# Attention scores of two heads together on the two halves of the array's rows, and bias addition with row maximum in one VectorE instruction

## What is computed

```
DILATED_PATTERNS = ((128, 1), (512, 4), (2048, 16))
def dilated_mixture_attention(q, k, v):
    outs, lses = [], []
    for window, dilation in DILATED_PATTERNS:
        o, lse = dilated_window_attention(q, k, v, window, dilation)
        ...
    wts = jax.nn.softmax(jnp.stack(lses, axis=0), axis=0)
    o = jnp.sum(wts[..., None] * jnp.stack(outs, axis=0), axis=0)
```

## Time and profile before

| | |
|---|---|
| median of 3 runs | 2277.92 us (2269.21 to 2280.78) |
| the profiled execution: time | 2277.48 us |
| the profiled execution: span | 2275.9 us |
| TensorE matmul busy | 2167.8 us (95% of the span) |
| VectorE, ScalarE busy | 1007.0 us, 633.6 us |
| mean granted TensorE clock | 0.98 |
| attention, first scores to last values matmul | 1215.3 to 1406.1 us |

### The profile page before, as it was taken

How to read it: one execution, slowest core, us unless ns; L and a number is a source line. 1 busy time by engine, 2 the same in 40 slices (tenths; PEclk the granted TensorE clock), 3 DMA queues, 4 the chain that set the end, 5 groups by cost and what they waited for, 6 DMA issues and landing times.

```text
span 2275.9 us, 25468 instructions
## 1 busy us (share of the span) xinstructions
PE 2167.8 (95%) x10465; PEld 1797.1 (79%) x10465; DVE 1007.0 (44%) x1109; ACT 633.6 (28%) x876; POOL 814.8 (36%) x320
## 2 busy tenths in 40 slices
PE   2999999999999999799999998979999999999998
PEld 2788888888877688678886787867888888878886
DVE  5776665666354456652504765142000000025656
ACT  4344444444210112322004755032000000012212
POOL 2333323323333355424541000333444444445552
PEclk9999999999999999989997999989999999999999
DMA  9111011011111111421110000321111111111131
GB/s 361 33 38 38 28 37 37 28 37 34 41 47 47 38 46 56 166 70 52 46 46 19 1 1 4 118 92 62 50 46 46 47 55 46 46 46 46 46 117 77
DMA packets 129974, 130.31 MB, mean 57 GB/s; under 512 B 6310, under 2 KB 103031, under 8 KB 128888
## 3 DMA queue, kind: packets, MB, share of 16 engines
q1 hardware_dynamic: 123208, 113.08, 15.5%
q10 hardware_dynamic: 6704, 16.36, 1.9%
HBM read 116.84 MB, written 12.58 MB: 57 GB/s over the span
## 4 chain that ended last, share of the span: by engine, by line
PE 91%; DVE 4%; ACT 3%; issue 1%; DMA 1%; ACTq 0%; DVEq 0%
PE psum L395 15%; PE psum L397 14%; PE psum L396 14%; PE psum L415 10%; PE psum L416 10%; PE psum L417 10%; PE psum L526 3%; PE psum L810 3%; PE psum L799 2%; PE psum L789 1%; PE psum L640 1%; PE psum L445 1%; DMA arena<-x 1%; DVE arena L1604 1%; PE psum L790 1%
## 5 line engine op out<-in xcount | busy, mean ns | idle before, releaser
L373 POOL TENSOR_TENSOR w_hi<-w_raw,ones 128x1024 fp32r<-128x1024 f32 x158 | 382.4, 2420 | 1422.3 <-PE psum L397 754.3
L395 PE MATMUL psum<-h_hi,w_hi 128*128 128x512 f32 x1472 | 586.9, 399 | 1.6 <-POOL w_lo L376 1.1
L397 PE MATMUL psum<-h_hi,w_lo 128*128 128x512 f32 x1472 | 575.3, 391 | 0.0
L396 PE MATMUL psum<-h_lo,w_hi 128*128 128x512 f32 x1472 | 574.7, 390 | 0.0
L376 POOL TENSOR_TENSOR w_lo<-w_raw,w_hi 128x1024 fp32r<-128x1024 f32 x158 | 432.4, 2737 | 12.4
L415 PE MATMUL psum<-w_hi,h_hi 128*128 128x512 f32 x1056 | 414.9, 393 | 16.4 <-DVE h_lo L1562 9.8
L416 PE MATMUL psum<-w_lo,h_hi 128*128 128x512 f32 x1056 | 413.7, 392 | 0.0
L417 PE MATMUL psum<-w_hi,h_lo 128*128 128x512 f32 x1056 | 413.3, 391 | 0.0
L395 PEld LDWEIGHTS psum<-h_hi,w_hi 128*128 128x128 f32 x1472 | 278.0, 189 | 60.2 <-issue 4.2
L397 PEld LDWEIGHTS psum<-h_hi,w_lo 128*128 128x128 f32 x1472 | 277.5, 188 | 59.1
L396 PEld LDWEIGHTS psum<-h_lo,w_hi 128*128 128x128 f32 x1472 | 278.0, 189 | 57.4 <-issue 2.4
(11 more groups left out here) (197 smaller groups left out, 2010.6 us busy)
## 6 DMA issues: line engine op xcount, KB each, us to landing
w_raw<-w_in SPq DMA_DIRECT2D x68, 512.0 KB, 3.8
w_raw<-w_out SPq DMA_DIRECT2D x24, 512.0 KB, 3.6
w_raw<-w_gate SPq DMA_DIRECT2D x22, 512.0 KB, 3.8
w_raw<-w_up SPq DMA_DIRECT2D x22, 512.0 KB, 3.8
w_raw<-w_down SPq DMA_DIRECT2D x22, 512.0 KB, 3.5
arena<-ada_w SPq DMA_DIRECT2D x8, 1024.0 KB, 13.9
x_mid<-arena ACTq DMA_DIRECT2D x16, 512.0 KB, 2.6
arena<-x_mid SPq DMA_DIRECT2D x16, 512.0 KB, 7.5
```

Of the source, the lines that this page charges most:

```text
L373: pool.tensor_tensor(w_hi[:, c, :].rearrange("p (a n) -> p a n", n=P), raw.rearrange("p (a n) -> p a n", n=P), unit_scale, ALU.mult).then_ ...
L395: pe.matmul(o, wh, xh, start=(k == 0), stop=False)
L396: pe.matmul(o, wh, xl, start=False, stop=False)
L397: return pe.matmul(o, wl, xh, start=False, stop=(k == KT - 1))
```

## The change

Two edits, both in the attention. First, `qk(n)` becomes `qk_pair(m)`: the scores of heads 2m and 2m + 1 are made by alternating matmuls, an even head on rows 0 to 63 of the array, an odd one on rows 64 to 127, each into a PSUM slot of its own. TensorE's loop goes over pairs: in one step stand `qk_pair(m)`, then `p_t` and `pv` for two heads. The pair waits until both slots are read (`s_moved` 2m). Second, L1741 and L1743 are replaced by one `tensor_tensor_reduce`, which writes the negated sum -(s + bias), and its minimum by row, which is the negated maximum. The exp takes scale -1 for it, and waits for `s_moved`; `max_done` is gone.

```diff
-            def qk(n):
-                i, h = n // AH, n % AH
-                if n >= 2:
-                    pe.wait_ge(s_moved, n - 1)
-                po = DH * (h % 2)
-                for c0 in range(0, (i + 1) * P, HALF):
-                    c1 = min(c0 + HALF, (i + 1) * P)
-                    o = two_banks(n % 2)[:, c0:c1]
-                    qh, ql = [x[po:po + DH, h // 2, i * P:(i + 1) * P] for x in (h_hi, h_lo)]
-                    kh, kl = [x[po:po + DH, 4 + h // 2, c0:c1] for x in (h_hi, h_lo)]
-                    pe.matmul(o, qh, kh, start=True, stop=False)
-                    pe.matmul(o, qh, kl, start=False, stop=False)
-                    mm = pe.matmul(o, ql, kh, start=False, stop=True)
-                mm.then_inc(s_full, 1)
+            def qk_pair(m):
+                i, p = 2 * m // AH, m % (AH // 2)
+                if m:
+                    pe.wait_ge(s_moved, 2 * m)
+                w = (i + 1) * P
+                for c0 in range(0, w, HALF):
+                    c1 = min(c0 + HALF, w)
+                    o = [two_banks(e)[:, c0:c1] for e in range(2)]
+                    qh, ql = [[x[DH * e:DH * e + DH, p, i * P:(i + 1) * P] for e in range(2)] for x in (h_hi, h_lo)]
+                    kh, kl = [[x[DH * e:DH * e + DH, 4 + p, c0:c1] for e in range(2)] for x in (h_hi, h_lo)]
+                    for e in range(2):
+                        pe.matmul(o[e], qh[e], kh[e], start=True, stop=False)
+                    for e in range(2):
+                        pe.matmul(o[e], qh[e], kl[e], start=False, stop=False)
+                    for e in range(2):
+                        mm = pe.matmul(o[e], ql[e], kh[e], start=False, stop=True)
+                        if c1 == w:
+                            mm.then_inc(s_full, 1)
...
-            for n in range(N + 3):
-                if n < N:
-                    qk(n)
-                if 0 <= n - N_SGU < SGU_G:
-                    sgu(n - N_SGU)
-                if 0 <= n - 2 < N:
-                    p_t(n - 2)
-                if 0 <= n - 3 < N:
-                    pv(n - 3)
+            for m in range(N // 2 + 2):
+                if m < N // 2:
+                    qk_pair(m)
+                for n in (2 * m, 2 * m + 1):
+                    if 0 <= n - N_SGU < SGU_G:
+                        sgu(n - N_SGU)
+                    if 0 <= n - 2 < N:
+                        p_t(n - 2)
+                    if 0 <= n - 3 < N:
+                        pv(n - 3)
...
-                    act.wait_ge(max_done, n + 1)
-                    A(probs[n % 4][:, 0:w], probs[n % 4][:, 0:w], ACT.Exp, bias=neg_max[:, n % 8:n % 8 + 1],
+                    act.wait_ge(s_moved, n + 1)
+                    A(probs[n % 4][:, 0:w], probs[n % 4][:, 0:w], ACT.Exp, scale=-1.0, bias=neg_max[:, n % 8:n % 8 + 1],
...
-                TT(probs[n % 4][:, 0:w], two_banks(n % 2)[:, 0:w], BIAS[:, PAGE - w:PAGE], ALU.add).then_inc(s_moved, 1)
-                dve.wait_ge(s_moved, n + 1)
-                dve.reduce_max(neg_max[:, n % 8:n % 8 + 1], probs[n % 4][:, 0:w], AX.X, negate=True).then_inc(max_done, 1)
+                dve.tensor_tensor_reduce(probs[n % 4][:, 0:w], two_banks(n % 2)[:, 0:w], BIAS[:, PAGE - w:PAGE], -1.0, F_BIG,
+                                         ALU.add, ALU.min, neg_max[:, n % 8:n % 8 + 1]).then_inc(s_moved, 1)
```

More of the change, by code:

```diff
@@ L48 @@
 F_MIN = 1e-19
+F_BIG = 3e38
 DH = 64
@@ L255, in program @@
         rope_step, trig_done, rope_done = sem("rope_step"), sem("trig_done"), sem("rope_done")
-        s_full, s_moved, max_done, p_done, pt_full, pt_done, pv_full, den_done, ao_done = (
-            sem("s_full"), sem("s_moved"), sem("max_done"), sem("p_done"), sem("pt_full"), sem("pt_done"),
+        s_full, s_moved, p_done, pt_full, pt_done, pv_full, den_done, ao_done = (
+            sem("s_full"), sem("s_moved"), sem("p_done"), sem("pt_full"), sem("pt_done"),
             sem("pv_full"), sem("den_done"), sem("ao_done"))
```

## The result

The changed kernel took 2239.14 us (median, 2233.75 to 2243.51), the kernel before, in the same comparison, 2274.88 us; the ratio is 0.9844 with a 95% interval of 0.9821 to 0.9866. So it is faster by 35.7 us. The profiled execution took 2239.2 us with a span of 2237.6 us, against 2275.9 before.

The account below looks back on a forecast made before the run. TensorE, busy 95% of the span, was taken as the bound. Savings of 21.6 + 5 = 26.6 us less 1.3 left 25.3, so 2277.5 - 25.3 = 2252 us; 8-in-10 range 2241 to 2267.

Parts of the forecast that it names:

- A pair's scores for the price of one head's: Scores on different array halves overlap, saving one visit (first score to first transpose) per pair: 21.6 us in blocks 4 to 7.
- the reserve: The gap between last value product and first score is passed half as often; left out of the sum, without a size.
- The trail of the second head: In pairs of score matmuls, 32 second heads trail by 0.04 us each, 1.3 us set against the saving.
- Blocks 2 and 3: Saving of 1.5 us each, limited by ScalarE's work and, in block 3, by a transpose waiting behind table loads.
- Blocks 0 and 1: Saving of 1 us each, as second transposes wait for ScalarE's copy of the first; block 0's visits alone would give 3.3.
- The joined instruction: On VectorE, takes the addition's 1.23 us plus 0.19 us accumulator read; brings nothing by itself in blocks 4 to 7.
- just under the cover of 5.6: Block 7: without joining, VectorE needs 5.3 us a pair, under 5.6 us of TensorE's transposes and value products.
- The coupled slots: Both slots must be empty before a pair starts; this wait costs nothing from block 4 on, only in blocks 0 to 3.
- The base: The starting time for the forecast: the profiled execution's 2277.48 us, 0.4 us from the median of 2277.92.
- no overlap: Rival: little or no overlap at 512 columns, only visit ends saved; 3 us less, 2274 us; chance 0.07.
- a doubled instruction: Rival: joining takes twice the addition's time, losing some 12 us, mainly in blocks 2 to 4; 2265 us; chance 0.08.
- The slower clock: Rival: TensorE's clock rises later or falls at block 3's longer wait; 10 to 20 us lost, 2262 to 2272; chance 0.08.

Follow-up runs that it names:

- e3: The changed kernel with both heads of a pair on rows 0 to 63, so the odd heads' scores come out different; 2263.66 us.
- e8: The kernel before with 11 matmuls filling TensorE's 2.4 us of idle time ahead of the first scores; 2266.07 us.
- the two kernels with the fill: The kernel before and the changed kernel, each with 11 matmuls ahead of the first scores; 2266.07 and 2238.61 us.
- e2: The kernel before with only addition and maximum joined, heads still scored one by one; 2269.99 us.
- e1: The changed kernel with scores still in pairs, but addition and maximum as two instructions again; 2241.62 us.
- e12: The changed kernel with the joined instruction executed twice for each head; 2253.41 us.
- e10: The changed kernel profiled once more, unchanged; 2237.60 us in one execution.
- e4: The kernel before with the spatial matmuls of steps 8 to 15 put in twos, nothing else changed; 2273.22 us.
- e5: The changed kernel with each head's three score matmuls listed together instead of alternating between the heads; 2238.05 us.

## Why the prediction came out as it did

The direction and the mechanism were right, the size was off by more than my range allowed. By its steps:

- **A pair's scores for the price of one head's.** Right, also at 512 columns and the higher clock, where I had no row: 1.58 us for a visit of two. e3 shows that this is the halves' doing (1.58 against 2.96 us a visit). The terms of blocks 4 to 7 were 21.6 us; measured 23.6. The difference is the reserve I had left out: behind the visit of two, the transposes and products of two heads take 7.05 - 1.58 = 5.47 us, where they took 2 x 2.81 = 5.62, which over 16 pairs is 2.4 us, near the 2.0 missing.
- **The trail of the second head, 1.3 us.** Wrong, it is too small to see: pairs of matmuls at 512 columns take at most 0.01 us longer than one.
- **Blocks 2 and 3, 1.5 us each.** 2.1 and 2.3 measured. ScalarE was the limit as read: it has 11.2 of 11.9 us of work in block 2 now. The transpose behind the table loads waits longer, 2.44 us.
- **Blocks 0 and 1, "I take 1 for each block".** This is the step that failed. Block 0 gave 1.8, block 1 6.9. I had priced block 1 at the clock that it had, and when I thought of the clock I let it only move against the change ("it could rise later"). It rose earlier: 27 us at the lower level became 14, in both profiles of either kernel. e8 prices that at 0.41 us for each us, so 13.7 us of it are an estimated 5.6 us; the two kernels with the fill put it at 36.7 - 30.8 = 5.9. Without these the time would have been near 2245 us, inside my range. The 1 us for block 1's own saving was too small as well: some 2.2.
- **The joined instruction.** The addition's 1.22 us, and 0.083 us for the accumulator read, under half of what I took from ScalarE's. It is worth 0.4 us alone (e2). With the pairs the profile without it is 3.0 and 2.5 us longer than the two of the changed kernel (e1), and 0.4 us of that lies from block 4 on. My sum that a pair without it would need 5.3 us, "just under the cover of 5.6", was borne out: the first three pairs of block 7 lose nothing in e1.
- **The coupled slots.** From block 4 on TensorE's matmuls waited 0.4 us in all for VectorE and its weight loads 0.9. e12 found the margin: at twice the instruction 13.4 us are lost, near the 12 us that I had given for that rival.
- **The base.** 2277.5 us was the profiled execution; the median of before in the comparison was 2274.9. That alone moves the forecast by 2.6 us.

Summed: 25.3 + 5.9 (block 1) + 2.0 (gaps) + 1.3 (trail) + 1.4 (blocks 2 and 3) + 0.8 (block 0) = 36.7 us, the attention's difference. Of the two terms of blocks 0 and 1, some 5.6 us are the clock's.

The rivals: no overlap is ruled out (e3), and a doubled instruction too (1221 ns). The slower clock went the other way in blocks 0 and 1. Its second half, a fall at the longer wait in block 3, is there in one of the two profiles of the changed kernel (e10), for 3.4 us and at a cost of 0.8 us (7.53 against 6.72). The wait's length alone doesn't decide it: with 2.20 us in the kernel before and 2.44 in the first profile of the changed kernel the clock stayed up, with 2.19 us in e4 and 2.42 in e10 it fell.

The Trainium skill's factor for four matmuls side by side ("TensorE: Matmul & The Clock Gate", Part 3, Measured speedup vs the span model), which would have made 2259 us, does not carry over to two halves here: 1.58 us for two visits against 1.58 for one. The Trainium skill says on the same page, in The mechanism, that matmuls start and end strictly in the order of the list; e5 and the earlier trace rows show starts in another order when the halves differ.

What exactly makes the clock rise in block 1 is not settled. The order of the list changes it (e4: 17 us instead of 27, without the overlap and the joined instruction; e3: 17, without the overlap; the changed kernel: 14), and so does what stood ahead of block 0 (e8: 10). More than that these runs don't tell.

## What to carry to other kernels

Two matmuls of 64 contraction rows on different halves of the array cost one here (1.58 us for two visits), so look for them wherever heads of width 64 come one after another, and count the saving only where TensorE has no idle time. When a change makes a sparse stretch at the lower clock denser, give the clock a price in both directions; here each us less at the lower level gave 0.41 us. Fewer instructions on an engine that isn't waited for buy cover and not time: the joined instruction alone took 46 us off VectorE and 0.4 us off the attention.

## What was not expected of the hardware

- TensorE takes a second head's matmuls on the other half ahead of the first head's later ones by itself: listed head by head, they start in twos 0.23 us apart (e5).
- Two overlapped score matmuls at 512 columns and the higher clock show no loss over 0.01 us: 0.39 to 0.40 us for a two, 0.23 us from two to two.
- The read of VectorE's accumulator takes 0.083 us, ScalarE's 0.186 us.
- 11 idle matmuls ahead of a sparse stretch shortened the time at the lower clock by 17 us in the kernel before (e8), though the clock still fell. It fell 3 us later and rose 3.6 us into block 1 where it had risen 16.2 us into it.
- At the end of a wait of 1.75 to 2.44 us in block 3 the clock fell for 3.4 us in seven of fourteen profiles, and in one of the two of the changed kernel.
